# The passage from projection to compression: stores on three signals, sample rows kept elsewhere, forget gates and the prompt's compression keys made earlier

## The reference

```python
p = jnp.einsum('btd,dn->btn', h, w_in)            # queries, keys, values, gates of all branches
q_a = rope(pq...); kv_cmp, kv_sel, kv_win = kv_rot(pcmp), kv_rot(psel), kv_rot(pwin)
logf = jax.nn.log_sigmoid(pf + b_forget)          # forget gates; cum = cumsum(logf) over the prompt

def compress(k, pos_emb, w):                      # for keys and for values, prompt and samples
    ch = k.reshape(B, L // 16, 16, G, dh)
    blocks = jnp.concatenate([ch[:, :-1], ch[:, 1:]], axis=2) + pos_emb
    return jnp.einsum('bnlgd,lde->bnge', blocks, w)
```

## Time and profile before

| | us |
|---|---|
| median of 3 runs (2833.75 to 2837.0) | 2835.87 |
| the profiled execution | 2833.41 |
| its span, first to last instruction | 2831.3 |
| TensorE busy in it | 2536.7 (90%) |
| VectorE / ScalarE / GpSimd busy | 936.6 / 539.4 / 642.7 |
| mean granted TensorE clock, as a share of full speed | 0.939 |

### The profile page before, as it was taken

How to read it: one execution, slowest core, us unless ns; L and a number is a source line. 1 busy time by engine, 2 the same in 40 slices (tenths; PEclk the granted TensorE clock), 3 DMA queues, 4 the chain that set the end, 5 groups by cost and what they waited for, 6 DMA issues and landing times.

```text
span 2831.3 us, 43445 instructions
## 1 busy us (share of the span) xinstructions
PE 2536.7 (90%) x13426; PEld 1963.6 (69%) x13426; DVE 936.6 (33%) x1905; ACT 539.4 (19%) x1360; POOL 642.7 (23%) x564
## 2 busy tenths in 40 slices
PE   4997888877899999999999877988779999999997
PEld 3885544444588888888888764444457887888886
DVE  3103465411222442333231145552112335222423
ACT  1013222212222211110000232222141221111100
POOL 0000022111132434443300001121111343444431
PEclk9999799878899999999999988997789999999998
DMA  6252334245122222221424233441532222222121
GB/s 194 74 138 69 98 111 130 62 127 160 60 90 90 67 83 90 90 71 62 144 84 134 69 101 100 118 131 43 170 105 90 74 76 89 90 80 77 55 86 47
DMA packets 288296, 270.89 MB, mean 96 GB/s; under 512 B 50882, under 2 KB 249746, under 8 KB 287810
## 3 DMA queue, kind: packets, MB, share of 16 engines
q1 hardware_dynamic: 271266, 258.43, 29.9%
q10 hardware_dynamic: 16800, 9.61, 1.1%
HBM read 258.36 MB, written 17.97 MB: 98 GB/s over the span
## 4 chain that ended last, share of the span: by engine, by line
PE 77%; SPq 8%; DVE 6%; issue 5%; ACT 2%; DMA 1%; POOL 0%; ACTq 0%; DVEq 0%; POOLq 0%
PE ps L1102 32%; PE ps L1228 9%; PE ps L628 6%; PE ps L696 5%; PE ps L697 5%; SPq L603 3%; PE ps L998 3%; PE ps L923 2%; PE ps L814 2%; SPq L600 2%; PE ps L862 1%; PE ps L661 1%; PE ps L662 1%; PE ps L703 1%; DVE arena L1873 1%
## 5 line engine op out<-in xcount | busy, mean ns | idle before, releaser
L1565 POOL TENSOR_SCALAR ring<-ring,rr,gnat 128x31 f32<-128x31 f32 (+2 forms) x192 | 101.3, 538 | 1026.9 <-DVE rr L1801 750.0
L1102 PE MATMUL ps<-hT,ring 128*128 128x260 f32 x1344 | 306.2, 385 | 6.3 <-DVE hT L1679 6.3
L1102 PEld LDWEIGHTS ps<-hT,ring 128*128 128x128 f32 x1344 | 257.3, 192 | 47.0 <-DVE hT L1679 7.1
L628 PE MATMUL ps<-cst,units 128*128 128x128 f32 x960 | 157.4, 297 | 62.7 <-DVE arena L1873 20.1
L1102 PE MATMUL ps<-hT,units 128*128 128x260 f32 x928 | 213.2, 382 | 0.0
L1102 PEld LDWEIGHTS ps<-hT,units 128*128 128x128 f32 x928 | 176.3, 190 | 27.1
L696 PE MATMUL ps<-hT,ring 128*128 128x260 f32 x640 | 193.2, 384 | 0.0
L697 PE MATMUL ps<-hT,ring 128*128 128x260 f32 x640 | 192.7, 383 | 0.0
L628 PEld LDWEIGHTS ps<-cst,units 128*128 128x128 f32 x960 | 113.4, 150 | 103.9 <-DVE arena L1873 37.7
L1102 PE MATMUL ps<-arena,units 128*128 128x260 f32 x704 | 158.1, 383 | 0.4 <-DVE arena L2036 0.4
L1102 PEld LDWEIGHTS ps<-arena,units 128*128 128x128 f32 x704 | 133.6, 190 | 21.6 <-issue 1.2
(11 more groups left out here) (319 smaller groups left out, 4376.3 us busy)
## 6 DMA issues: line engine op xcount, KB each, us to landing
ring<-in_w_in SPq DMA_DIRECT2D x20, 2048.0 KB, 8.6
units<-in_cache_fox_kv SPq DMA_DIRECT2D x256, 128.0 KB, 2.2
units<-in_cache_sb_kv SPq DMA_DIRECT2D x256, 128.0 KB, 2.2
ring<-in_w_ffn_gate SPq DMA_DIRECT2D x22, 1024.0 KB, 5.4
ring<-in_w_ffn_up SPq DMA_DIRECT2D x22, 1024.0 KB, 8.0
ring<-in_w_ffn_down SPq DMA_DIRECT2D x16, 1408.0 KB, 6.3
units<-in_cache_nsa_cmp_kv SPq DMA_DIRECT2D x128, 128.0 KB, 2.6
units<-in_cache_nsa_sel_kv SPq DMA_DIRECT2D x256, 64.0 KB, 1.9
```

The lines of the kernel that those rows point to most:

```text
L628: return nc.tensor.transpose(o, i, ident[0:n, 0:n])
L1102: last = mm(ps[:, bank, 0:H2], w[:, k, :], a[:, k, :], start=first and k == 0, stop=True, skip_group_check=True)
L1565: last = nc.gpsimd.tensor_scalar(p, p, one, gnat[:, i, c:c + 1], ALU.mult, ALU.mult)
```

## The change

- `natS` moves from `arena` to the unused upper part of weight slot 0 (`ring`), which holds the compression weights below it.
- The stores of key and value rows are counted on three semaphores: the first seven (`early_dma`, to the first stick-breaking key tile), the next five (`key_dma`, to the last forget-attention key tile), and the rest with those of the samples and gates (`out_dma`). In the first round, the copies of turned(0,0) into `KC` wait for `early_dma`, those of turned(0,1) for `key_dma`; `new_ready` is given after the compression's last step and waited for at the start of VectorE's attention.
- GpSimd copies the prompt's own keys and values into `KC`, ahead of its attention work: the keys after `early_dma`, the values after `key_dma`, each copy waiting for the one before.
- VectorE takes the last step of the forget gates during the projection (at i = 18), and TensorE sums them right after the last tile's multiplication, before the last two tiles are transposed.
- VectorE's work on the samples' rows becomes `new_rows`, after turned(0,1); ScalarE's stores of them come after turned(0,1), those of the gates after turned(1,0). TensorE's first two steps wait for the copies of the last two tiles out of banks 6 and 7.

```diff
+EARLY, LATE = NAT.index(SBK) + 1, NAT.index(FXK + 1) + 1
...
-        ropet, knat, natS = ar(0, T), ar(T, len(NATV) + 2, TT * P), ar(T + 7 * 512 + 512, len(NAT), P)
+        ropet, knat = ar(0, T), ar(T, len(NATV) + 2, TT * P)
+        natS = ring[:, 0, 2048:2048 + len(NAT) * P].rearrange("p (a b) -> p a b", b=P)
...
                 post(NT - 1)
+                cumulate(l)
                 nat(NT - 2)
                 nat(NT - 1)
...
-                pe.wait_ge(sems["nat_ev"], at(pe, "nat_ev", l, len(NAT)))
-                pe.wait_ge(sems["new_ev"], at(pe, "new_ev", l, 1))
...
-                        if step >= 2:
+                        if step < 2:
+                            pe.wait_ge(sems["nat_ev"], at(pe, "nat_ev", l, len(NAT) - 1 + step))
+                        else:
...
-                    act.dma_start(dst, src).then_inc(sems["out_dma"], 16)
+                    act.dma_start(dst, src).then_inc(sems["early_dma" if n < EARLY else "key_dma" if n < LATE else "out_dma"], 16)
...
                 def turned(q, kv):
+                    if q == 0:
+                        name = ("early_dma", "key_dma")[kv]
+                        act.wait_ge(sems[name], at(act, name, l, PER[name]))
...
                 for q in range(4):
                     for kv in range(2):
                         turned(q, kv)
+                        if (q, kv) == (0, 1):
+                            store_rows()
+                        elif (q, kv) == (1, 0):
+                            store_gates()
+                act.wait_ge(sems["sig_dma"], at(act, "sig_dma", l, 32))
+                act.wait_ge(sems["out_dma"], at(act, "out_dma", l, PER["out_dma"]))
+                act.sem_inc(sems["new_ready"], 1)
...
+                pool.wait_ge(sems["rope_done"], at(pool, "rope_done", l, ROPE.index(CMPK) + 1))
+                pool.wait_ge(sems["proj_ev"], at(pool, "proj_ev", l, CMPV + 1))
+                for kv in range(2):
+                    name = ("early_dma", "key_dma")[kv]
+                    pool.wait_ge(sems[name], at(pool, name, l, PER[name]))
+                    apart(pool)
+                    for g in range(G):
+                        for a in range(2):
+                            n = 6 * kv + 3 * g + a + 1
+                            nc.gpsimd.tensor_copy(KC[a * DH:(a + 1) * DH, kv, g, :, W_OWN:W_POS],
+                                                  PT[g * DH:(g + 1) * DH, CMPK + kv, 0:SEQ].rearrange("p (n m a) -> p a m n", m=8, a=2)[:, a]).then_inc(sems["kc_part"], 1)
+                            pool.wait_ge(sems["kc_part"], at(pool, "kc_part", l, n))
...
+                        nc.gpsimd.tensor_copy(KC[:, kv, g, :, W_POS:W_POS + 2], posL[:, :].rearrange("p (n m) -> p m n", m=8)).then_inc(sems["kc_part"], 1)
...
             def compress(l):
-                dve.wait_ge(sems["new_ready"], at(dve, "new_ready", l, 1))
-
                 def turned(q, kv):
+                    if q == 0:
+                        name = ("early_dma", "key_dma")[kv]
+                        dve.wait_ge(sems[name], at(dve, name, l, PER[name]))
...
                 turned(0, 0)
                 turned(0, 1)
+                new_rows(l)
```

More of the change, by code:

```diff
@@ L217, in layer_counts @@
              new_ps=1, new_ev=1, gate_ps=1, gate_ev=1, gate_sig=1, lf_abs=1, lf_ln=1, lf_done=1, cum_ps=1, cum_ev=1,
-             sig_dma=32, lf_in=16 * NS * NPG, out_dma=16 * (len(NAT) + len(STORED) + 2), q_ev=1, new_ready=1,
+             sig_dma=32, lf_in=16 * NS * NPG, early_dma=16 * EARLY, kc_part=12, key_dma=16 * (LATE - EARLY), out_dma=16 * (len(NAT) - LATE + len(STORED) + 2), q_ev=1, new_ready=1,
              kc_own=2, ck_ev=1, cvt_ps=1, cvt_ev=1,
@@ L663, in tile, with cumulate @@
                 return last
+            def cumulate(l):
+                pe.wait_ge(sems["lf_done"], at(pe, "lf_done", l, 1))
+                for t in range(TT):
+                    last = mm(ps[0:4, 4, t * P:SEQ], lfn[:, t, :], cum_fwd[:, 0:SEQ - t * P], start=t == 0, stop=True, skip_group_check=True)
+                last.then_inc(sems["cum_ps"], 1)
             def project(l):
@@ L728, in project @@
                 last.then_inc(sems["new_ps"], 1)
-            def cumulate(l):
-                pe.wait_ge(sems["nat_ev"], at(pe, "nat_ev", l, len(NAT)))
-                pe.wait_ge(sems["new_ev"], at(pe, "new_ev", l, 1))
[L734 to L737, removed]
             def compress(l):
-                cumulate(l)
                 def turned(q, kv):
@@ L1357, in project, with compress @@
                     stored += 1
[L1358 to L1379, removed]
+                return store_new
+            def compress(l, store_new):
                 def turned(q, kv):
+                    if q == 0:
+                        name = ("early_dma", "key_dma")[kv]
+                        act.wait_ge(sems[name], at(act, name, l, PER[name]))
                     for u in range(4):
@@ L1388, in turned, with store_rows, store_gates @@
                         last.then_inc(sems["kt_ea"], 1)
+                def store_rows():
+                    act.wait_ge(sems["new_ev"], at(act, "new_ev", l, 1))
+                    for name, n, w in STORED:
+                        store_new(name, n, w)
+                def store_gates():
+                    act.wait_ge(sems["lf_done"], at(act, "lf_done", l, 1))
+                    with nc.allow_non_contiguous_dma(reason="gates and log-forget values: a few kilobytes"):
+                        act.dma_start(out["p_logf"].rearrange("l a (t p) h -> (l a) p t h", p=P)[dl[0]], lfn[:, :, :]).then_inc(sems["out_dma"], 16)
+                        act.dma_start(out["s_logf"].rearrange("l b s h -> l (b s) h")[dl[0]], lfs[:, :]).then_inc(sems["out_dma"], 16)
+                        act.wait_ge(sems["gate_sig"], at(act, "gate_sig", l, 1))
+                        act.dma_start(g64[:, :], gsmp[:, 0:24]).then_inc(sems["sig_dma"], 16)
+                        act.dma_start(l32[:, :], lfs[:, :]).then_inc(sems["sig_dma"], 16)
                 for q in range(4):
@@ L1531, in _ @@
                 l = layer[0] = in_layers(act, i)
-                project(l)
-                compress(l)
+                compress(l, project(l))
                 attend(l)
@@ L1712, in project, with new_rows @@
                         nat(i - 1)
+                    if i == 18:
+                        dve.wait_ge(sems["gate_ev"], at(dve, "gate_ev", l, 1))
+                        dve.wait_ge(sems["lf_ln"], at(dve, "lf_ln", l, 1))
+                        v.scalar_tensor_tensor(lfn[:, :, :], lfn[:, :, :], 0.0, lft[:, :, :], ALU.min, ALU.subtract)
+                        v.scalar_tensor_tensor(lfs[:, :], lfs[:, :], 0.0, lfst[:, :], ALU.min, ALU.subtract).then_inc(sems["lf_done"], 1)
+                dve.wait_ge(sems["cum_ps"], at(dve, "cum_ps", l, 1))
+                v.tensor_scalar(ncum[:, :], ps[0:4, 4, :], -1.0, None, ALU.mult).then_inc(sems["cum_ev"], 1)
+            def new_rows(l):
                 dve.wait_ge(sems["new_ps"], at(dve, "new_ps", l, 1))
@@ L1720, in project @@
                     v.tensor_copy(vnew[:, i, :], natS[0:NS, NAT.index(t), :])
[L1721 to L1725, removed]
                 for g in range(G):
```

8 lines of the change are left out of this document (6 added, 2 removed).

## The result

The changed kernel took 2806.98 us (median of 4 executions, 2803.59 to 2808.76) beside 2836.41 for the kernel before; the ratio is 0.9892 [0.9876, 0.9908]. The profiled execution took 2806.2, its span is 2804.4.

The account below looks back on a forecast made before the run. The prediction held that SyncE's load queue paces the stage and step 4 sets its start. Gains of 11.6 + 11.4 + 0.9 = 23.9 us gave 2835.87 - 23.9 = 2812.0 us, range 2807 to 2824.

Parts of the forecast that it names:

- The chain to step 4: From TensorE ready after the projection, through gate sum, 22 transposes and copies, to step 4's transposes: 8.39 us; 11.6 us saved in layer 0.
- step 4: The transposes that free the load queue's first place, so their start sets the first page load; forecast 238.6 against 250.21.
- Full clock: TensorE no longer idles ahead of the steps, so gate sum takes 2.32 us and the queue starts 0.44 sooner per layer.
- the two ends: Full clock throughout the passage, gain 23.9 us, or the lower level of 1.2 GHz throughout, gain 18.8 us.
- The queue in hand: SyncE's load queue has 2.7 us to spare behind step 4, so it doesn't notice the moved work.
- Step 12's end: Step 12 ends 16.4 us behind the queue's start; the seventeenth load, which needs it, is due at 19.1.
- The slow rival: GpSimd's copies come too late and TensorE waits at compressed(0,1); at 8 us a copy 2870 us; chance 0.05.
- the sharing rival: GpSimd and VectorE exclude each other, stopping VectorE's copies of steps 0 to 4: 5.6 us a layer, 2823.2; chance 0.08.
- The third rival: The passage isn't the start of the pace, or its time is given back in attention: 2835.9 us; chance 0.05.
- The moved work: Samples' rows and ScalarE's nine issues behind step 4: VectorE's copies 1.2 us late, within the queue's 2.7 in hand.
- the runs' own spread: Part of the range's lower end: 1.6 us, half of 2833.75 to 2837.0.
- handovers that I priced too high: Part of the range's lower end: 3 us for waits between engines in the passage that might prove shorter.

Follow-up runs that it names:

- the experiments that make TensorE idle 5.85 us or more ahead of the steps: Changed kernel with the prompt's own keys copied by ScalarE before step 0: 2820.85 us; or with samples' rows and nine small DMAs first: 2821.88 us.
- the experiment that uses them up: Changed kernel plus eight linked VectorE adds behind the samples' rows, before the compression of the pages: 2820.14 us, ratio 0.993.
- the slot alone: Kernel before with only the samples' rows (`natS`) put into the weight slot: 2835.86 us, ratio 1.0002.

## Why the prediction was right in its mechanism and off at the low end

The forecast was 2812.0, the range 2807 to 2824; 2806.98 lies 5.0 below the one and 0.02 below the end of the other. By its steps:

- **The chain to step 4.** Forecast 8.39 behind TensorE's readiness, measured 242.73 - 234.65 = 8.08 (in layer 1 1605.57 - 1597.49, the same). The sum of the gates and the transposes overlap by a little, 2.24 and 2.46 from start to start instead of 2.32 and 2.64, and the first copy begins 0.64, not 0.70, behind its transposes; from there to step 4 it is 2.74, forecast 2.73. (The prediction's "8 steps" in 3.49 us are 8 copies, which make four steps; its prices of a copy and of a step are right.) From step 4 to the first load it is 0.83, forecast 0.85. Together 24.5 us instead of 23.9: right.
- **Full clock.** The sum took 2.31 us in both layers; the choice between the two ends was right, and the experiments that make TensorE idle 5.85 us or more ahead of the steps show the other case (1.97 for eight transposes).
- **The queue in hand.** Step 12's end was put 16.4 behind the first load; its transposes begin at 15.53, which puts their end at 16.2 (four take 0.65). VectorE is late behind the samples' rows by 252.12 - 251.19 = 0.9 us, forecast 1.2 (step 8's transposes at 250.49, a copy 0.70 later). The 2.7 us in hand are 2.7 in layer 0 and 2.4 in layer 1 by the experiment that uses them up.
- **GpSimd.** A copy took 608 ns, 0.75 us from one start to the next, against 0.9 taken with its wait. The keys' copies began as said during the projection, at 200.19; those of the values 4.87 us behind the sum's start, a microsecond later than I had put them, and ended at 243.09, 11.5 ahead of compressed(0,1) at 254.55. Off the path, as said; doubled, they still are. The slow rival falls, and the sharing rival for these copies, though VectorE's copies within SBUF were seen to wait. The third rival, that the time is given back in attention, falls by the table: the rows behind the first load are no longer than before beyond their scatter.
- **The moved work.** The first load's place is right and no wait was added. The experiments give the two moved parts their price: 6.11 a layer for the keys, 7.4 to 7.6 for the samples' rows and small stores.
- **The step that failed** is the last one, the range's lower end: "1.6 for the runs' own spread (half of 2833.75 to 2837.0) and 3 for handovers that I priced too high". The handovers took 0.6 of their 3; the spread was sized too small. Three executions were too few to show it. Sets of twelve, sixteen, eighteen and twenty-three of the kernel before lay between 2827.13 and 2845.85, 14 of the changed one between 2803.35 and 2815.21, and the three comparisons gave 29.4, 27.4 and 23.6 us, 26.8 in the mean. Behind the sum stood also the tacit step that nothing outside the passage moves: the end is 1.8 us shorter in every profile of the changed kernel, and the merge 3.5 to 4 shorter in them than in the profile I had read, but short in that of the slot alone as well. A third part is the median, carried over as 2.46 above the profiled execution: the changed kernel's was 0.78 above its own. So of the 5.0, 1.7 is the median, 0.6 the passage, and 2.7 what moved outside it in the two profiles (the merge and the end 5.5 shorter, the other rows 3.1 longer, and 0.3 outside the span). Why the merge and the end moved stays open. With the end, 24.5 + 1.8 = 26.3 is what I would now forecast.

## What to carry to other kernels

Where a stage is paced by a queue, ask which instruction frees its first slot and count only what stands ahead of that one; everything else may move behind it as far as the queue has time in hand, and that time can be measured by making the moved engine late. Idle time of TensorE ahead of such a chain is paid for twice when its clock falls, and a delay put ahead of it comes out longer than it is: 5.84 us of adds made 7.6 here. Before a range is given, a spread of three executions should be taken for a lower bound: here eighteen spread four times as far.

## What was not expected of the hardware

After the same idle time of 2.8 us near the end, the granted clock stayed at 0.50 for some 6.8 us in three profiles and for some 3.4 in eleven, the same in each repeat of a kernel; in the merge for some 17 in two and some 10 in twelve. By estimate, at half of the difference, these are worth 1.7 and some 3.4 us, more than many edits. And GpSimd's strided copy of 64 by 256 was as even as VectorE's from PSUM, 602 to 629 ns over 48 of them, with VectorE busy beside it; a copy of VectorE's within SBUF that began beside it took 0.63 us instead of 0.21.
